# Dilation-16 attention of heads 8 to 15 of layer 0 from stored rows, off TensorE

## The chip, the cores and the metric

One Trainium2 chip; the kernel runs on one core. The metric is device time in microseconds (us), the median of several runs. The kernel before takes 2405.73 us (three runs, 2405.4 to 2406.24).

## What is computed

Four layers run one after the other on x of 256 tokens by 2048 columns (batch 1). Layer 0, which the change touches, is dilated attention with 16 heads of 128 columns and three patterns:

```
DSA_PATTERNS = ((128, 1), (512, 4), (2048, 16))     # (window, dilation)
h = x @ w_in                                        # 2048 x 20480: q, k, v for 3 groups of 2048, then z
for g, (window, dilation) in enumerate(DSA_PATTERNS):
    q = apply_rope(qkv[:, :, g, 0], cos, sin)
    k = apply_rope(qkv[:, :, g, 1], cos, sin)
    o, l = dilated_window_attention(q, k, qkv[:, :, g, 2], window, dilation)   # out, log-sum-exp
wts = jax.nn.softmax(jnp.stack(lses, axis=0), axis=0)
o = jnp.einsum('gbsh,gbshd->bshd', wts, jnp.stack(outs, axis=0).astype(jnp.float32))
y = o.reshape(B, S, DSA_WIDTH).astype(x.dtype) * jax.nn.silu(z)
return y @ w_out
```

Query t of a pattern sees keys t, t-d, t-2d, ... up to its window. With dilation 16 and 256 tokens there are 16 residue classes of 16 tokens each, and causal attention runs inside a class. Weighting three softmaxes by their log-sum-exp is the same as one softmax over the keys of all three patterns together. Layers 1 (latent attention), 2 and 3 are not changed.

## The kernel before, in words

**Projections.** TensorE multiplies float32 data as a high and a low part (float32r): x as xh and xl (both in xx), each weight as whi and wlo. SyncE brings weights in units of 128x4x512 float32 (1 MB) into four buffers `raw`. ScalarE casts a half unit (128x1024) to whi (`split`, L1387), VectorE subtracts it from raw to get wlo (L2030), and TensorE may use the half when wlo is done. Both splits of a half are issued three halves ahead of TensorE (AHEAD = 3); whi and wlo have four buffers. SyncE issues unit u when the wlo of unit u-4 is done.

**Slabs.** The input projection of layer 0 goes by pairs of heads, eight times: six *blocks* (`block_by_rows`, L729 and L730: 256 columns of q or k, weights stationary, result transposed) and two *projects* (`project`, L696 to L698: 512 columns, x stationary), one for v of groups 0 and 1, one for v of group 2 and z. Two banks of PSUM are used in turn. ScalarE copies a slab out (L1636, L1641, L1646), and VectorE adds the part with xl to a block (L2411).

**Work beside the slabs.** All engines walk the same generators: a half is two *steps*, so a block is 8 steps and a project 16. At steps `beside` lets the attention of the pair before run (`heads0`: scores L972, max L2267, exp L1529, transposes L977, product with v L983, result L2385), and from step 54 of a pair's 80 the rotation of the six new blocks (`rope0`), one every three steps: VectorE multiplies by the sine (L2368, twice 64x512), GpSimd by the cosine (L2940, 128x512), VectorE adds (L2372). For one head the scores are two sets (one for each 128 tokens) of 256 + 128 + 128 columns: full block for dilation 1 and the masked 128 of the same half for each of the dilations 4 and 16. Every instruction waits on semaphores, and the order on each engine is as the program is written; nothing is reordered at run time.

The layer ends with the output product (`last_product`), beside which the last pair's heads run.

Of the kernel before, what the change touches and what calls it, by code (L numbers as in the profile page):

```python
# [14 lines left out]
P = 128  # L15
D = 2048
# [23 lines left out]
ROWS_AT = (40, 44, 48, 52)  # L40
# [62 lines left out]
def lanes(gates, delta, lru, gated):  # L103

    lane = [[(0, gates()), (40, lru(0)), (86, lru(2)), (132, delta(0)), (250, delta(2))],
            [(48, lru(1)), (114, lru(3)), (180, delta(1)), (298, delta(3))],
            [(302, gated(0)), (324, gated(1)), (356, gated(2)), (388, gated(3))]]
    tick = 0  # L110
    while any(lane):
        for side in lane:
            if side and tick >= side[0][0] and next(side[0][1], "over") == "over":
                del side[0]
        tick += 1
        yield

# [43 lines left out]
def build_program(nc, a, out, layers=(0, 1, 2, 3)):  # L161
    assert tuple(layers) == (0, 1, 2, 3)
    ctx = ExitStack()
    with ctx:
# [82 lines left out]
        e0_a, s0_d = marks("e0_a", "out*8"), marks("s0_d", "sum*6")  # L247
        p0_a = marks("p0_a", "vb z")
        p0_d = marks("p0_d", "t0 r0 t1 r1 t2 r2 t3 r3 t4 r4 t5 r5 z")
        p0_g = marks("p0_g", "cos*6")  # L250
# [43 lines left out]

        class L0:
            c = Carve()
            h = c(10, TB, HALF)
            t1, t2 = c(2, S), c(2, S)
# [4 lines left out]
            sm, pt, mask = c(TB, N), c(TB, N), c(TB, N)  # L303
            c.at = 14592 + 1152
# [7 lines left out]
            BLOCKS = [(0, 0), (0, 1), (1, 0), (1, 1), (2, 0), (2, 1), (0, 2), (1, 2), (2, 2), (3, 0)]  # L312
# [125 lines left out]

        def xt_turn(layer, g, tb=None):
# [100 lines left out]
        def layers_weights():  # L540
            for pair in range(8):
                cols = [pair * HALF + (3 * g + t) * D for g, t in L0.BLOCKS]
                for c in cols[0:6]:
                    yield from (by_block(L0.w, c, j) for j in range(2))
                for n in (6, 8):
                    yield from (by_columns(L0.w, cols[n:n + 2], j) for j in range(4))
# [67 lines left out]
        def sync(sp):  # L614
            first = [src for _, halves in list(weights())[0:2] for _, src in halves]
            for g in range(8):
                c = slice(g * S, (g + 1) * S)
                sp.dma_start(x[:, :, c], a["x"][0].rearrange("(p t) d -> p t d", t=TB)[:, :, c]).then_inc(x_in[g], 16)
                sp.dma_start(first_piece(raw, g), first[g // 2][:, 2 * (g % 2):2 * (g % 2) + 2]).then_inc(first_in[g], 16)
            for u, (_, halves) in enumerate(weights()):  # L620
# [14 lines left out]
                if u in decays_at:  # L635
# [3 lines left out]
                    sp.dma_start(flat(L3.lane[pair % 2].B), row(decays[2 * pair], 2 * S)).then_inc(dec_in[pair], 16)  # L639
                for dst, src in halves:  # L640
# [10 lines left out]
                if u in ROWS_AT:  # L651
                    q = ROWS_AT.index(u)
                    sp.wait_ge(*xt_p.at(7, "t"))
# [13 lines left out]
        def tensor(pe):  # L667
# [293 lines left out]
            def rope0(pair):  # L961
                yield from turns(7)

            def heads0(pair):
                yield
                for hh in range(2):
                    def scores():
                        for tb in range(TB):
                            for g in range(3):
# [5 lines left out]
                    def turned():  # L975
                        for b in range(8):
                            m = pe.transpose(flat4[:, b * P:(b + 1) * P], L0.sm[:, b // 4, b % 4 * P:(b % 4 + 1) * P], ident[:, :])  # L977
                        return m

                    def pv():  # L980
                        for tb in range(TB):
                            for b, (g, kb) in enumerate(((0, 0), (0, 1), (1, tb), (2, tb))):
                                m = pe.matmul(ps[:, Q + 3, tokens[tb]], L0.pt[:, tb, b * P:(b + 1) * P],  # L983
                                              L0.vb[:, g, kb, hh * P:(hh + 1) * P], start=b == 0, stop=b == 3)
                        return m
                    if hh == 0:
                        pe.wait_ge(*p0_d.at(pair, "r5"))
                    yield from attend(2 * pair + hh, scores, turned, pv, 3, hh == 1)

            def beside0(pair, tables_):  # L990
                return beside(paced(heads0(pair - 1), 3) if pair else tables_, 54, paced(rope0(pair), 3))
# [7 lines left out]
            for pair in range(8):  # L999
                side = beside0(pair, tables())  # L1000
                for s in range(8):
                    if s >= 2:
                        pe.wait_ge(*s0_d.at(pair, f"sum{s - 2}"))
                    elif pair:
                        pe.wait_ge(*e0_a.at(pair - 1, f"out{6 + s}"))
                    if s < 6:
                        block_by_rows(side, bank0(s), pair + s == 0)
                    else:
                        project(side, N, bank0(s),
                                then=turning_y(0, [[hd_d.at(11, "fin"), e0_a.at(7, "out6")]] + 5 * [[]]) if pair + s == 14 else None)  # L1010
                run(side)
            last_product(0, heads0(7), [yt_d.at(5, "lo"), e0_a.all(8)], [], [hd_d.at(15, "fin")])


# [358 lines left out]
        def scalar(act):  # L1373
# [222 lines left out]
            def rope0(pair):  # L1596
                yield from turns(7)

            def heads0(pair):
                act.wait_ge(*e0_a.all(pair + 1))  # L1600
                if pair:
                    act.wait_ge(*hd_p.at(2 * pair - 1, "pv"))
                for g in range(3):
# [4 lines left out]
                act.activation(L0.zs, L0.h[:, 9], ACT.Tanh).then_inc(*p0_a.up("z"))  # L1608
                yield
                for hh in range(2):  # L1610
                    yield from attend(2 * pair + hh, [L0.sm[:, 0], L0.sm[:, 1]], P ** -0.5, flat(L0.pt),
                                      flat4[:, 0:TB * N], 3, hh == 1)

            def beside0(pair, tables_):
                return beside(paced(heads0(pair - 1), 3) if pair else tables_, 54, paced(rope0(pair), 3))
# [10 lines left out]
            for pair in range(8):  # L1626
                side = beside0(pair, tables())
                for s in range(8):
                    b = bank0(s)
                    if s < 6:  # L1630
                        unit(side)
                        unit(side)
                        act.wait_ge(half_done, half[0])
                        if pair:
                            act.wait_ge(*p0_d.at(pair - 1, f"r{s}"))
                        act.copy(L0.h[:, s], ps[:, b:b + 2, 0:S]).then_inc(*e0_a.up(f"out{s}"))  # L1636
                        continue
                    project(side, then=turning_y(0) if pair + s == 14 else None)
                    act.wait_ge(half_done, half[0])
                    if s == 6:  # L1640
                        act.copy(L0.h[:, 6:8].rearrange("p b t c -> p t b c"),  # L1641
                                 ps[:, b:b + 2, :].rearrange("p t (b c) -> p t b c", b=2)).then_inc(*e0_a.up("out6"))
                    else:
                        if pair:
                            act.wait_ge(*p0_d.at(pair - 1, "z"))
                        act.copy(L0.h[:, 8], ps[:, b:b + 2, 0:HALF])  # L1646
                        act.activation(L0.h[:, 9], ps[:, b:b + 2, HALF:N], ACT.Copy, scale=0.5).then_inc(*e0_a.up("out7"))
                run(side)
# [368 lines left out]
        def vector(dve):  # L2017
# [337 lines left out]
            def rope0(pair):  # L2355

                for n in range(6):
                    dve.wait_ge(*s0_d.at(pair, f"sum{n}"))
                    if n == 0:
                        if pair == 0:  # L2360
                            dve.wait_ge(*rope_a.at(0, "tab"))
                            dve.wait_ge(*m0_g.at(0, "same2"))
                        else:
                            dve.wait_ge(*hd_p.at(2 * pair - 1, "sc"))
                    else:
                        dve.wait_ge(*p0_d.at(pair, f"r{n - 1}"))
                    for a_, b_ in ((slice(0, 64), slice(64, P)), (slice(64, P), slice(0, 64))):
                        m = dve.tensor_tensor(L0.t2[a_], L0.h[b_, n], bc(L0.sina[b_], 1, 2), ALU.mult)  # L2368
                    m.then_inc(*p0_d.up(f"t{n}"))
                    dve.wait_ge(*p0_d.at(pair, f"t{n}"))  # L2370
# [3 lines left out]
                yield  # L2374

            def heads0(pair):
                dve.wait_ge(*p0_a.at(pair, "z"))
                dve.scalar_tensor_tensor(out=L0.zs, in0=L0.zs, scalar=1.0, in1=L0.h[:, 9],
                                         op0=ALU.add, op1=ALU.mult).then_inc(*p0_d.up("z"))
                yield  # L2380
                for hh in range(2):
                    def fin(rden):
# [6 lines left out]
                    parts = [(ps[:, Q + tb, :], L0.mask[:, tb], L0.sm[:, tb]) for tb in range(TB)]  # L2389
                    yield from attend(2 * pair + hh, parts, P ** -0.5, fin, 3, hh == 1)  # L2390

            def beside0(pair, tables_):
                return beside(paced(heads0(pair - 1), 3) if pair else tables_, 54, paced(rope0(pair), 3))
# [10 lines left out]
            for pair in range(8):  # L2404
                side = beside0(pair, tables())
                for s in range(8):
                    if s < 6:
                        unit(side)
                        unit(side)
                        dve.wait_ge(*e0_a.at(pair, f"out{s}"))  # L2410
                        dve.tensor_tensor(L0.h[:, s], L0.h[:, s], ps[:, bank0(s):bank0(s) + 2, S:N], ALU.add) \  # L2411
                            .then_inc(*s0_d.up(f"sum{s}"))
                    else:
# [678 lines left out]
```

## Time and profile before

| what | value |
|---|---|
| median of three runs | 2405.73 us |
| span of the profiled execution | 2404.2 us, its ends about 1.5 us inside a run's time |
| TensorE busy | 2395.8 us (100%) |
| VectorE, ScalarE, GpSimd busy | 1478.8, 1186.4 and 151.6 us |
| granted TensorE clock | 1.000 over the span |
| DMA | 418.26 MB, mean 174 GB/s |

A busy time is the time in which an engine had an instruction running. TensorE is the engine to watch: it has an instruction running all the time, so any time it gains or loses is the kernel's. The other engines only matter where they make it wait. In a timeline row the first number is the start, the second the duration, then engine, line, operation, output and inputs, shape, and xN for N instructions merged; square brackets hold idle time before it and who ended it.

### The profile page before, as it was taken

The page shows a single profiled execution, that of the slowest core. Times are in us where ns is not written, and L with a number is a line of the kernel's source. Part 1 is how long each engine was busy: PE and PEld are TensorE (multiplying, and loading weights), DVE is VectorE, ACT ScalarE, POOL GpSimd, SP SyncE. Part 2 cuts the span into 40 slices and gives each one's busy share as a digit, 9 for nine tenths or more (in the row PEclk, how much of TensorE's full clock was granted, in tenths as well). Part 3 has the DMA queues.
Part 4 walks back from the last instruction along what each step waited for, and adds up shares of the span by engine and source line. Part 5 has one row for each costly group of instructions (what it writes and reads, how often), then busy time and mean ns, then how long its engine had stood idle before and what let it go on. Part 6 is the DMA issues. An engine that isn't in the chain of part 4 may idle for free.

```text
span 2404.2 us, 31347 instructions
## 1 busy us (share of the span) xinstructions
PE 2395.8 (100%) x12574; PEld 2043.6 (85%) x12574; DVE 1478.8 (62%) x1986; ACT 1186.4 (49%) x1645; POOL 151.6 (6%) x130
## 2 busy tenths in 40 slices
PE   9999999999999999999999999999999999999999
PEld 8888888888888888878899878888888888888887
DVE  6747575757575757575556576555445566757754
ACT  5454444444444444445455456455444358745543
POOL 0201010101010101000000000000000010000000
PEclk9999999999999999999999999999999999999999
DMA  8555555555555555556654556556555565534344
GB/s 265 178 173 191 196 185 169 186 168 186 168 186 169 186 167 176 194 164 201 188 142 136 193 160 201 179 178 193 177 178 171 175 196 172 157 120 128 126 140 140
DMA packets 370366, 418.26 MB, mean 174 GB/s; under 512 B 28262, under 2 KB 300876, under 8 KB 369708
## 3 DMA queue, kind: packets, MB, share of 16 engines
q1 hardware_dynamic: 368876, 409.36, 53.3%
q0 software_dynamic: 1344, 6.89, 0.8%
q8 instruction: 99, 1.62, 0.3%
q14 instruction: 47, 0.39, 0.0%
HBM read 414.09 MB, written 2.11 MB: 173 GB/s over the span
## 4 chain that ended last, share of the span: by engine, by line
PE 97%; DVE 1%; ACT 1%; issue 0%; POOL 0%; DVEq 0%; ACTq 0%; POOLq 0%
PE ps L696 19%; PE ps L698 19%; PE ps L697 19%; PE ps L730 15%; PE ps L729 7%; PE ps L1260 2%; PE ps L771 2%; PE ps L983 1%; PE ps L972 1%; PE ps L1037 1%; PE ps L1035 1%; PE ps L1036 1%; PE ps L977 1%; PE ps L802 1%; PE ps L804 0%; PE ps L803 0%
## 5 line engine op out<-in xcount | busy, mean ns | idle before, releaser
L2030 DVE TENSOR_TENSOR wlo<-raw,whi 128x1024 fp32r<-128x1024 f32 (+1 forms) x756 | 938.6, 1251 | 617.8 <-ACT whi L1387 615.0
L1387 ACT CAST whi<-raw 128x1024 fp32r<-128x1024 f32 x762 | 789.1, 1041 | 713.8 <-PE ps L698 536.1
L696 PE MATMUL ps<-whi,xx 128*128 128x512 f32 x2060 | 820.3, 398 | 0.0
L698 PE MATMUL ps<-whi,xx 128*128 128x512 f32 x2060 | 803.6, 390 | 0.0
L697 PE MATMUL ps<-wlo,xx 128*128 128x512 f32 x2060 | 802.2, 389 | 0.0
L730 PE MATMUL ps<-xx,whi 128*128 128x512 f32 x1536 | 539.4, 396 | 0.0
L698 PEld LDWEIGHTS ps<-whi,xx 128*128 128x128 f32 x2060 | 386.7, 188 | 82.5
L697 PEld LDWEIGHTS ps<-wlo,xx 128*128 128x128 f32 x2060 | 387.5, 188 | 75.5
L696 PEld LDWEIGHTS ps<-whi,xx 128*128 128x128 f32 x2060 | 387.2, 188 | 74.5
L729 PE MATMUL ps<-xx,wlo 128*128 128x256 f32 x1440 | 406.0, 282 | 0.0
L730 PEld LDWEIGHTS ps<-xx,whi 128*128 128x128 f32 x1536 | 286.3, 188 | 63.2 <-DVE wlo L2030 0.3
L729 PEld LDWEIGHTS ps<-xx,wlo 128*128 128x128 f32 x1440 | 271.6, 189 | 2.5 <-issue 0.5
L2940 POOL TENSOR_TENSOR work<-work 128x512 f32<-128x512 f32 x48 | 96.7, 2014 | 827.6 <-DVE work L2372 627.3
L1529 ACT ACTIVATE work<-work,small 128x128 f32<-128x128 f32 (+1 forms) x80 | 44.4, 555 | 143.2 <-DVE small L2270 143.2
L2368 DVE TENSOR_TENSOR work<-work 64x512 f32<-64x512 f32 x96 | 88.5, 922 | 2.1
L1636 ACT COPY work<-ps 128x512 f32<-128x512 f32 x48 | 28.0, 584 | 60.0 <-PE ps L730 60.0
L2411 DVE TENSOR_TENSOR work<-work,ps 128x512 f32<-128x512 f32 x48 | 32.9, 686 | 36.8 <-ACT work L1636 36.8
L1260 PEld LDWEIGHTS ps<-work 128*128 128x128 f32 x384 | 49.5, 191 | 6.2 <-ACT work L1943 1.6
L1260 PE MATMUL ps<-work 128*128 128x128 f32 x384 | 51.1, 276 | 0.8 <-ACT work L1943 0.4
L2267 DVE CUSTOM_DVE_ANT_0 work<-ps,work 128x128 f32<-128x128 f32 (+1 forms) x80 | 36.0, 487 | 21.0 <-PE ps L972 15.6
L1035 PE MATMUL ps<-xx,whi 128*128 128x256 f32 x160 | 48.1, 301 | 0.0
L1037 PE MATMUL ps<-xx,whi 128*128 128x256 f32 x160 | 45.2, 283 | 0.0
(436 smaller groups left out, 1917.1 us busy)
## 6 DMA issues: line engine op xcount, KB each, us to landing
raw<-in_dsa_w_in SPq DMA_DIRECT2D x316, 512.0 KB, 4.5
raw<-in_ev_w_in SPq DMA_DIRECT2D x144, 512.0 KB, 4.6
raw<-in_od_w_in SPq DMA_DIRECT2D x96, 512.0 KB, 4.6
raw<-in_mla_w_in SPq DMA_DIRECT2D x48, 512.0 KB, 4.5
raw<-in_dsa_w_out SPq DMA_DIRECT2D x32, 512.0 KB, 4.7
raw<-in_mla_w_out SPq DMA_DIRECT2D x32, 512.0 KB, 4.8
raw<-in_ev_w_out SPq DMA_DIRECT2D x32, 512.0 KB, 4.7
raw<-in_od_w_out SPq DMA_DIRECT2D x32, 512.0 KB, 4.9
```

The lines of the kernel that those rows point to most:

```text
L696: pe.matmul(o, xh[:, k, tokens[tb]], hi, start=start and s + l == 0, stop=False)
L697: pe.matmul(o, xh[:, k, tokens[tb]], lo, start=False, stop=False)
L698: m = pe.matmul(o, xl[:, k, tokens[tb]], hi, start=False, stop=stop and s + l == 2)
L729: pe.matmul(ps[:, bank + c, 0:S], lo[:, t, cols], xh[:, k, :], start=False, stop=False)
L730: m = pe.matmul(ps[:, bank + c, :], hi[:, t, cols], xx[:, :, k, :], start=k == 0, stop=k == KT - 1)
L1035: pe.matmul(o, hi, xh[:, k, :], start=first and g != 1, stop=False)
L1037: m = pe.matmul(o, hi, xl[:, k, :], start=False, stop=last and g != 0)
L1260: m = pe.matmul(ps[:, bank, n * P:(n + 1) * P], left[:, n, :], right[:, n, :], start=True, stop=True)
L1387: act.copy(half_of_weights(h)[0][:, :, 0:n] if n > FEW else few_high(h, n), whole_half(raw[:, u % 4, 2 * (h % 2):2 * (h % 2) + 2], n)).the ...
L2030: dve.tensor_tensor(lo[:, :, 0:n] if n > FEW else few_low(h, n), whole_half(raw[:, h // 2 % 4, 2 * (h % 2):2 * (h % 2) + 2], n), hi.bitcas ...
L2368: m = dve.tensor_tensor(L0.t2[a_], L0.h[b_, n], bc(L0.sina[b_], 1, 2), ALU.mult)
L2940: pool.tensor_tensor(L0.t1, L0.h[:, n], bc(L0.cosa, 1, 2), ALU.mult).then_inc(*p0_g.up(f"cos{n}"))
```

## The change

Heads 8 to 15 (pairs 4 to 7) lose their dilation-16 part on TensorE; it is computed once, for all eight heads, on GpSimd and VectorE.

- **Slabs.** After the first block come six new 512-column projects ("row" slabs): q, k and v of group 2 for heads 8 to 15 (1024 columns each). Pairs 4 to 7 have four blocks instead of six, one v project each, and one z project for two pairs. In the whole layer 48 blocks and 16 projects become 40 blocks and 20 projects.
- **Rows.** The q and k rows are rotated in row form on VectorE (`row_ropes`: sine twice 128x512, cosine 128x1024, sum 128x1024, four times), stored to memory (`far_rows`) and read back by `by_sequence` with a partition for each residue class and head (128 of them) and 16 tokens of 128 numbers along it.
- **Products.** For each distance (lag 0 to 15) GpSimd multiplies q and k in pieces of at most 8 tokens (1024 numbers in a partition; 24 pieces, 136 tokens in all), and VectorE sums each piece to its scores. The reduce of piece n stands at step 115 + 6n of the layer. After the exponential (step 260) GpSimd multiplies probabilities and v in the same pieces, and VectorE adds them up at step 279 + 6n. GpSimd's piece n waits for VectorE's piece n-2.
- **Back.** The sums go to memory, come back into y with one maximum and denominator for each token and head, and `attend0` joins them with the other two patterns.
- **Rotation.** In `rope0` the product with the cosine moves from GpSimd to VectorE, for all pairs; it starts at step 150 in pair 0 (which has 176 steps), at 54 in pairs 1 to 3 and at 31 in pairs 4 to 7.
- **Loads of x for the end of the layer** move from units 40 to 52 to units 118 to 130; x holds q, k and v until then.

```diff
+STEPS0 = (176, 80, 80, 80, 64, 48, 64, 48)
+ROPE_AT = (150, 54, 54, 54, 31, 31, 31, 31)
+PIECES = [(lag, n, min(8, LAGS - lag - n)) for lag in range(LAGS) for n in range(0, LAGS - lag, 8)]
+PIECE_STEPS = 6
+FAR_AT, FAR_EXP_AT, FAR_SUM_AT, FAR_OUT_AT = 112, 260, 263, 276
+STORES_AT = {16: 0, 18: 1, 22: 2, 26: 3, 30: 4, 34: 5}
+FAR_LOADS_AT, FAR_VALUES_AT, FAR_STORES_AT, FAR_BACK_AT = 29, 71, 112, 114
...
-                            for g in range(3):
+                            for g in range(3 if pair < 4 else 2):
                                 q, k = L0.qk[:, 2 * g, hh, tokens[tb]], L0.qk[:, 2 * g + 1, hh, tokens[tb] if g else slice(0, S)]
...
                     for a_, b_ in ((slice(0, 64), slice(64, P)), (slice(64, P), slice(0, 64))):
                         m = dve.tensor_tensor(L0.t2[a_], L0.h[b_, n], bc(L0.sina[b_], 1, 2), ALU.mult)
...
-                    dve.wait_ge(*p0_g.at(pair, f"cos{n}"))
-                    dve.tensor_tensor(L0.qk[:, n], L0.t1, L0.t2, ALU.add).then_inc(*p0_d.up(f"r{n}"))
+                    dve.tensor_tensor(L0.t1, L0.h[:, n], bc(L0.cosa, 1, 2), ALU.mult).then_inc(*done.up(f"c{n}"))
+                    dve.wait_ge(*roped0(pair, f"c{n}"))
+                    dve.tensor_tensor(L0.qk[:, n], L0.t1, L0.t2, ALU.add).then_inc(*done.up(f"r{n}"))
                     yield
...
+            def far0():
+                to = steps()
+                for n, (lag, i, size) in enumerate(PIECES):
+                    yield from to(FAR_AT + PIECE_STEPS * n + 3)
+                    dve.wait_ge(*far_g.at(0, f"q{n}"))
+                    dve.tensor_reduce(L0.far_s[:, lag + i:lag + i + size, lag], L0.tmp[n % 2][:, 0:size], AX.X, ALU.add) \
+                        .then_inc(*far_d.up(f"s{n}"))
...
+                for n, (lag, i, size) in enumerate(PIECES):
+                    if lag:
+                        yield from to(FAR_OUT_AT + PIECE_STEPS * n + 3)
+                        o = L0.far_o[:, lag + i:lag + i + size]
+                        dve.wait_ge(*far_g.at(0, f"o{n}"))
...
+                        dve.tensor_tensor(o, o, L0.tmp[n % 2][:, 0:size], ALU.add).then_inc(*far_d.up(f"a{n}"))
...
+            for n, (lag, i, size) in enumerate(PIECES):
+                if n >= 2:
+                    pool.wait_ge(*far_d.at(0, f"s{n - 2}"))
+                pool.tensor_tensor(L0.tmp[n % 2][:, 0:size], L0.far_q[:, lag + i:lag + i + size], L0.far_k[:, i:i + size],
+                                   ALU.mult).then_inc(*far_g.up(f"q{n}"))
```

How the order moves. VectorE in the rotation of pair 0, before: from its first block on, L2030 is the low split, L2368 the sines, L2372 the sum of a rotated block.

```order
L2368 TENSOR_TENSOR work<-work 64x512 x2
L2372 TENSOR_TENSOR work<-work 128x512
L2030 TENSOR_TENSOR wlo<-raw,whi 128x1024
L2368 TENSOR_TENSOR work<-work 64x512 x2
L2372 TENSOR_TENSOR work<-work 128x512
L2030 TENSOR_TENSOR wlo<-raw,whi 128x1024 x2
```

The same place in the changed program (L2189 is the low split, L2530 the sines, L2532 the cosine, L2534 the sum, L2566 the reduce of a piece of GpSimd's products):

```order
L2530 TENSOR_TENSOR work<-work 64x512 x2
L2532 TENSOR_TENSOR work<-work 128x512
L2534 TENSOR_TENSOR work<-work 128x512
L2566 TENSOR_REDUCE work<-y 128x8
L2189 TENSOR_TENSOR wlo<-raw,whi 128x1024
L2530 TENSOR_TENSOR work<-work 64x512 x2
L2532 TENSOR_TENSOR work<-work 128x512
L2534 TENSOR_TENSOR work<-work 128x512
L2189 TENSOR_TENSOR wlo<-raw,whi 128x1024 x2
```

Between the same low splits VectorE now has the cosine product, and at every sixth step a reduce.

GpSimd behind the masks, before (the cosine products of all 48 blocks, then the loads for the layer norm):

```order
L2940 TENSOR_TENSOR work<-work 128x512 x48
L2944 DMA work<-in_ln_g 128x2048
L2945 DMA work<-in_ln_b 128x2048
```

And now (L3203 multiplies q and k):

```order
L3203 TENSOR_TENSOR y<-x 128x1024 x3
L3203 TENSOR_TENSOR y<-x 128x896
L3203 TENSOR_TENSOR y<-x 128x1024
L3203 TENSOR_TENSOR y<-x 128x768
L3203 TENSOR_TENSOR y<-x 128x1024
```

The 48 cosine products are gone, and 24 products of q and k and 24 of probabilities and v, of up to twice their size, stand in their place.

## Rows read from the trace of the kernel before

**Rows 1.** The page: busy time (us, share of the span, instructions), and chain by engine

```profile
PE 2395.8 (100%) x12574; PEld 2043.6 (85%) x12574; DVE 1478.8 (62%) x1986; ACT 1186.4 (49%) x1645; POOL 151.6 (6%) x130
...
PE 97%; DVE 1%; ACT 1%; issue 0%; POOL 0%; DVEq 0%; ACTq 0%; POOLq 0%
```

**Rows 2.** Waits of TensorE, its longest: us in total, times, longest

```profile
PE ps L777 <- POOL ident L2909: 1.6, 1, 1.6
```

**Rows 3.** Timeline of TensorE at the borders of slabs, second pair

```profile
151.59 0.28 PE L732 MATMUL ps<-xx,wlo 128*128 128x256 f32 x1
...
162.89 0.28 PE L732 MATMUL ps<-xx,wlo 128*128 128x256 f32 x1
...
176.74 0.28 PE L732 MATMUL ps<-xx,wlo 128*128 128x256 f32 x1
...
187.84 0.28 PE L732 MATMUL ps<-xx,wlo 128*128 128x256 f32 x1
...
198.91 0.39 PE L696 MATMUL ps<-whi,xx 128*128 128x512 f32 x1
...
242.45 0.39 PE L730 MATMUL ps<-xx,whi 128*128 128x512 f32 x1
```

**Rows 4.** Timeline of TensorE, one head: scores, transposes, product with v

```profile
248.08 1.92 PE L972 MATMUL ps<-work 128*128 128x256 f32 x12
249.75 0.36 PE L729 MATMUL ps<-xx,wlo 128*128 128x256 f32 x1
...
262.34 1.03 PE L977 MATMUL ps<-ident,work 128*128 128x128 f32 x8
263.13 0.36 PE L729 MATMUL ps<-xx,wlo 128*128 128x256 f32 x1
...
267.39 1.95 PE L983 MATMUL ps<-work 128*128 128x128 f32 x16
269.17 1.92 PE L972 MATMUL ps<-work 128*128 128x256 f32 x12
```

**Rows 5.** Timeline of VectorE in the rotation of the second pair

```profile
208.40 1.23 DVE L2030 TENSOR_TENSOR wlo<-raw,whi 128x1024 fp32r<-128x1024 f32 x1 [1.49 <-ACT whi L1387]
209.66 1.39 DVE L2368 TENSOR_TENSOR work<-work 64x512 f32<-64x512 f32 x2
211.08 0.69 DVE L2372 TENSOR_TENSOR work<-work 128x512 f32<-128x512 f32 x1
211.69 1.22 DVE L2030 TENSOR_TENSOR wlo<-raw,whi 128x1024 fp32r<-128x1024 f32 x1
212.94 2.37 DVE L2368 TENSOR_TENSOR work<-work 64x512 f32<-64x512 f32 x2
215.34 0.69 DVE L2372 TENSOR_TENSOR work<-work 128x512 f32<-128x512 f32 x1
...
235.50 4.62 DVE L2030 TENSOR_TENSOR wlo<-raw,whi 128x1024 fp32r<-128x1024 f32 x4
```

**Rows 6.** Timeline of GpSimd: a cosine product beside VectorE, one alone

```profile
211.92 2.14 POOL L2940 TENSOR_TENSOR work<-work 128x512 f32<-128x512 f32 x1 [71.91 <-DVE work L2372]
...
257.11 1.30 POOL L2940 TENSOR_TENSOR work<-work 128x512 f32<-128x512 f32 x1 [23.50 <-DVE work L2411]
```

**Rows 7.** Timeline of TensorE: starts of three halves of that project

```profile
207.07 0.39 PE L696 MATMUL ps<-whi,xx 128*128 128x512 f32 x1
...
215.23 0.39 PE L696 MATMUL ps<-whi,xx 128*128 128x512 f32 x1
...
236.99 0.39 PE L696 MATMUL ps<-whi,xx 128*128 128x512 f32 x1
```

**Rows 8.** VectorE's groups by form: count, busy us, mean ns

```profile
L2528 DVE TENSOR_TENSOR work<-work,small 128x1024 f32<-128x1024 f32 x4 | 4.9, 1219 | 0.0
...
L2521 DVE TENSOR_REDUCE small<-work 128x8 f32<-128x1024 f32 x4 | 4.8, 1210 | 0.0
```

**Rows 9.** DMA issues of two kinds: count, size, median us to landing

```profile
raw<-in_dsa_w_in SPq DMA_DIRECT2D x316, 512.0 KB, 4.5
...
out_x<-x SPq DMA_DIRECT2D x3, 512.0 KB, 6.7
```

More of the change, by code:

```diff
@@ L116, in lanes, with joined @@
         yield
+def joined(n, side, more):
+    for _ in range(n):
+        next(side, None)
+        next(more, None)
+        yield
+    yield from side
 def in_turn(*sides):
@@ L437, in head_scales, with gate0, far_scales @@
             return [small[:, 16 + 8 * (h % 4) + 2 * i:18 + 8 * (h % 4) + 2 * i] for i in range(4)]
+        def gate0(pair):
+            return L0.h[:, 9] if pair < 4 else L0.hz[:, :, pair % 2 * HALF:(pair % 2 + 1) * HALF]
+        def far_scales(h):
+            return [small[:, 64 + 4 * (h % 4) + 2 * i:66 + 4 * (h % 4) + 2 * i] for i in range(2)]
         def xt_turn(layer, g, tb=None):
@@ L975, in turned @@
                     def turned():
[L976 to L977 removed]
+                        n = 4 if pair < 4 else 3
+                        for b in range(TB * n):
+                            m = pe.transpose(flat4[:, b * P:(b + 1) * P], L0.sm[:, b // n, b % n * P:(b % n + 1) * P], ident[:, :])
                         return m
@@ L998, in tensor @@
             keep_warm(1, 3)
[L999 to L1012, printed above, removed]
+            for n, (kind, i, block) in enumerate(slabs0):
+                if n == 0 or pair_of(kind, i) != pair_of(*slabs0[n - 1][0:2]):
+                    if n:
+                        run(side)
+                    side = beside0(pair_of(kind, i))
+                if n >= 2:
+                    pe.wait_ge(*read0(*slabs0[n - 2]))
+                if kind == "block":
+                    block_by_rows(side, bank0(n), n == 0)
+                else:
+                    project(side, N, bank0(n),
+                            then=turning_y(0, [[hd_d.at(11, "fin"), read0(*slabs0[n - 1])]] + 5 * [[]]) if n == len(slabs0) - 1 else None)
+            run(side)
+            last_product(0, heads0(7), [yt_d.at(5, "lo"), n0_a.all(4)], [], [hd_d.at(15, "fin")])
             def norms():
@@ L1625, in scalar @@
                 piece(g)
[L1626 to L1642, printed above, removed]
-                    else:
[L1644 to L1648, printed above, removed]
@@ new lines, in scalar @@
+            for n, (kind, i, block) in enumerate(slabs0):
+                if n == 0 or pair_of(kind, i) != pair_of(*slabs0[n - 1][0:2]):
+                    if n:
+                        run(side)
+                    side = beside0(pair_of(kind, i))
+                if kind == "block":
+                    unit(side)
+                    unit(side)
+                else:
+                    project(side, then=turning_y(0) if n == len(slabs0) - 1 else None)
+                evicted0(kind, i, block, bank0(n))
@@ L2355, in rope0 @@
             def rope0(pair):
-                for n in range(6):
-                    dve.wait_ge(*s0_d.at(pair, f"sum{n}"))
+                done = p0_d if pair < 4 else n0_d
+                for n in range(6 if pair < 4 else 4):
+                    dve.wait_ge(*sum0(pair, n))
                     if n == 0:
@@ L2403, in vector @@
                 piece(g)
[L2404 to L2413, printed above, removed]
-                        project(side, then=turning_y(0) if pair + s == 14 else None)
-                run(side)
+            for n, (kind, i, block) in enumerate(slabs0):
+                if n == 0 or pair_of(kind, i) != pair_of(*slabs0[n - 1][0:2]):
+                    if n:
+                        run(side)
+                    side = beside0(pair_of(kind, i))
+                if kind == "block":
+                    unit(side)
+                    unit(side)
+                    dve.wait_ge(*out0(i, f"out{block}"))
+                    dve.tensor_tensor(L0.h[:, block], L0.h[:, block], ps[:, bank0(n):bank0(n) + 2, S:N], ALU.add) \
+                        .then_inc(*(s0_d if i < 4 else t0_d).up(f"sum{block}"))
+                else:
+                    project(side, then=turning_y(0) if n == len(slabs0) - 1 else None)
+            run(side)
             last_product(0, heads0(7), ALPHA)
```

315 lines of the change are left out of this document (268 added, 47 removed).

## The prediction

> **What bounds the kernel now.** I read the page first: TensorE is busy for 2395.8 of 2404.2 us and carries 97% of the chain of waits [rows 1]. Then its waits: the longest is 1.6 us, at the very start [rows 2]. So the kernel is TensorE's instruction stream, end to end. The change is therefore worth what it takes out of that stream, less whatever new waiting it puts into it, and TensorE can wait for one thing above all in layer 0: the low part of the next half of weights, which VectorE makes. The timelines of TensorE and VectorE say how near that wait already is.
>
> In the project of the second pair TensorE begins a half at 207.07 us [rows 7]. VectorE makes its low split from 208.40 to 209.63 [rows 5], for the half that is three further on, which starts at 215.23 [rows 7]: 5.6 us to spare. Then the rotation begins, and eight splits later VectorE starts one at 235.50, done (a quarter of 4.62 us) at 236.7 [rows 5]; TensorE starts on that half at 236.99 [rows 7]. The 5.6 us have shrunk to 0.3. Eight halves are 236.99 - 215.23 = 21.76 us, 2.72 each; VectorE needed 27.1 us for what it does in them, of the 21.8 + 5.6 = 27.4 it may take. It does not delay TensorE, but nothing is left.
>
> Why so long? One rotation costs 1.42 us of sines (209.66 to 211.08) and 0.61 of sum (211.08 to 211.69), 2.03 in all [rows 5]. The next one's sines take from 212.94 to 215.34, 2.40 us, 0.98 longer, and meanwhile GpSimd multiplies by the cosine (211.92 to 214.06) [rows 5, 6]. That product takes 1.30 us when VectorE is idle [rows 6]. Of the 2.14 us beside VectorE, about a microsecond is waiting for the split that ends at 212.91, and then VectorE waits about a microsecond for GpSimd. So a product of 512 numbers costs a busy VectorE 1.0 us. Eight splits of 1.21, six rotations of 2.03 and five such holds make 9.7 + 12.2 + 5.0 = 26.9 us, against the 27.1 measured: this bookkeeping is right to a few tenths, and I use it below.
>
> The Trainium skill ("SBUF — State Buffer", section "Who interferes with whom") says the same of a VectorE instruction with two inputs in SBUF against a GpSimd instruction that reads SBUF: one has a lock for its whole instruction and the other stands still; a reduce does not take part. The trace agrees on the split and the sines (0.98 us); no row here shows a reduce beside GpSimd. By the page's whole-instruction rule a hold would be the full 1.30 us, which would make the sum below some 2.5 us longer.
>
> **What TensorE loses.** For each of heads 8 to 15 a quarter of the score columns (256 of 1024), two of eight transposes and two of eight products with v go. The three groups take 249.75 - 248.08 = 1.67, 263.13 - 262.34 = 0.79 and 269.17 - 267.39 = 1.78 us [rows 4]; a quarter of each is 0.42 + 0.20 + 0.44 = 1.06, and for eight heads 8.5 us. Eight blocks become four projects, with the same number of weight columns. Blocks without a head beside them take 162.89 - 151.59 = 11.30 and 187.84 - 176.74 = 11.10, two projects 242.45 - 198.91 = 43.54 [rows 3]: 8 x 11.2 - 4 x 21.77 = 89.6 - 87.1 = 2.5 us. Together **-11.0 us**. All of it is on the path, since TensorE never waits.
>
> **What VectorE gets.** In the rotation each block now carries the cosine, 0.69 us by the sum of the same shape [rows 5], and the GpSimd hold of 1.0 goes. With a small allowance for its wait on that product I take 2.75 us for a rotation. Alone that would be 9.7 + 16.5 = 26.2 us in eight halves: 0.7 better than before. But the pieces of the far attention fall into the same steps. A reduce of 1024 numbers takes 1.21 us, an elementwise sum 1.22 [rows 8]: 0.15 us for a token of 128. And each reduce or sum releases GpSimd's next product but one, which VectorE, then behind, runs into. The row gives 0.98 us for 512 numbers, 0.25 a token; I take 0.26. The bounds are 0 (the product falls where VectorE is idle or reducing) and 0.325 (the whole 1.30).
>
> The pieces by step, over the eight halves from the first rotated block, against 27.4 us:
>
> - Pair 0 (steps 150 on): reduces of 8, 5 and 8 tokens, 3.2 us; products of 8, 4 and 8, 5.2. 26.2 + 8.4 = 34.6: TensorE waits 7.2.
> - Pair 1 (230 on): reduces of 4 and 3, 1.05; products of 2 and 1, 0.8. 28.05: 0.7.
> - Pair 2 (310 on): sums of 8 and 5, 2.0; products of 8 and 4, 3.1; a product of 5 that holds back the first split, 0.9. 32.2: 4.8.
> - Pair 3 (390 on): sums of 5, 4 and 3, 1.8; products of 3 and 2, 1.3. 29.3: 1.9.
>
> That is 14.6 us of waiting, from 3.4 with no holds to about 17 with whole ones. Pairs 4 to 7 rotate four blocks each with the far part over (it ends at step 417), so nothing is late there.
>
> Outside the rotations a full piece every six steps asks for three splits (3.6), a reduce (1.2), a hold (2.1) and the sums of blocks (0.5): 7.4 of 8.2 us. That fits, but with 0.8 us to spare, and beside a head VectorE also waits for ScalarE. I add 1 us for such places (0 to 8).
>
> **What else moves.** The row rotations (four times two sines, cosine and sum, 1.4 + 1.2 + 1.2 us) are spread over steps 34 to 78 with a split between the parts, where GpSimd does nothing; each part is under the 5.6 us to spare: nothing. The joined heads have a few more small instructions on VectorE, in pairs where the rotation is shorter by two blocks: nothing. SyncE gets 13 transfers and waits in front of the weights. Its waits are for work that is over eight or more steps (11 us) earlier, by the steps of the program. The transfers cost time only if weights land late: a unit is issued when the splits four units back are done, by the program some six halves (6 x 2.72 = 16.3 us) before ScalarE casts it, and lands in 4.5 us [rows 9]. At unit 29 two loads of 1 MB in rows of 512 bytes go first. A 512 KB store takes 6.7 us with its latency [rows 9]; four times that is 27 us as the worst, and 0 if they overlap like weights. I take 0: only 11.8 us of delay would begin to show in the cast, and a further 5.6 in TensorE.
>
> **Sum.** -11.0 + 14.6 + 1.0 = +4.6 us. The profiled execution spans 2404.2 us with 1.5 around it in the median of 2405.73; both shift alike: **2410 us**. What this kernel's measurement can tell from no change is about 0.2%, 4.8 us: 2400.9 to 2410.5. The forecast is thus a small loss at the upper end of no change.
>
> **Rivals.**
> 1. *The holds do not come* (18%): GpSimd's products fall into gaps and reduces. For it: only half of VectorE's time is taken on average. Against it: in the rotation VectorE has no gap at all [rows 5], and GpSimd is released by VectorE itself. Time: 2405.7 - 11.0 + 3.4 = 2398, faster.
> 2. *GpSimd's pieces are dearer than its cosine products* (10%): with strided rows or a broadcast factor at twice the time, the holds are 0.52 a token. In the rotations 40 tokens more by 0.26 add 10; outside them six steps ask for 9.5 of 8.2 us, 1.3 late on each of some 20 full pieces, about 25. Time: about 2445. It decides from the point where sum and hold of a piece pass 4.1 us. Against it: type and operation are those of rows 6.
> 3. *The far loads delay the weights* (7%): 27 + 4.5 - 21.9 = 9.6 us of waiting at step 112, on top of the rest: 2420. For it: rows of 512 bytes; against it: 2 MB is two units' worth.
>
> **How the numbers follow.** The forecast's own case (65%) spans 2404 to 2417; I give 36% of all to its part within 0.2% and 29% to the part above. With rival 1 nearly all faster (17%, 1% same) and rivals 2 and 3 slower: faster 17%, same 37%, slower 46%. The range from 2398 to 2421 takes in rivals 1 and 3 and the bounds of the holds.
>
> **What would show it.** TensorE's busy share in layer 0 should fall, with waits for the low split (nothing before) near steps 150 to 170 and 310 to 330, some 7 and 5 us, less near 230 and 390. VectorE should be without idle there, with splits and sines of 2 to 3 us beside GpSimd; a product of 1024 numbers on GpSimd should take about 2.4 us alone and 3 to 4 beside VectorE; reduces should keep 1.2. Blocks and projects should keep 11.2 and 21.8 us. The prediction is wrong if TensorE never waits (rival 1), if its waits lie between the rotations (rival 2), or if ScalarE waits for a transfer near unit 29 (rival 3). No row shows TensorE waiting for microseconds, so whether its granted clock then stays at 1.000 is not priced; a fall would add to the loss.

## The result and the profile after

The changed kernel takes **2410.61 us** (18 runs, 2408.82 to 2411.68), the kernel before 2405.89 in the same comparison (18 runs, 2405.33 to 2406.38). The ratio is 1.0019, 95% interval 1.0012 to 1.0025: a loss of 4.7 us, small, but the interval leaves out 1. The forecast was 2410.0. The profiled execution of the changed kernel took 2408.82 us, with a span of 2406.7, and is the quickest of its 18; why most are 1.8 us above it is told with the last experiment.

The page, with the busy times (us, share of the span, instructions) and the chain of waits by engine, beside [rows 1]:

```profile
PE 2387.6 (99%) x12366; PEld 2027.7 (84%) x12366; DVE 1537.5 (64%) x2100; ACT 1181.0 (49%) x1642; POOL 150.2 (6%) x131
...
PE 91%; DVE 5%; issue 2%; ACT 1%; DMA 0%; POOL 0%; SPq 0%; DVEq 0%; ACTq 0%
```

TensorE has less to do than before, by 2395.8 - 2387.6 = 8.2 us, and yet the span is 2.5 us longer. The chain, 97% TensorE before, now runs 5% of the way over VectorE. The longest wait of TensorE (us in total, times, longest), beside [rows 2]:

```profile
PE ps L808 <- DVE wlo L2189: 9.4, 8, 2.3
```

It is new: eight times TensorE stands still for a low split. All eight lie beside the rotations of pairs 0 to 3. The timeline of TensorE shows two of them in pair 0, and below them three groups of matmuls of a head (start, duration, line, tiles, count; in brackets the wait ahead of it):

```profile
210.02 0.39 PE L808 MATMUL ps<-whi,xx 128*128 128x512 f32 x1
...
242.86 0.50 PE L808 MATMUL ps<-whi,xx 128*128 128x512 f32 x1 [1.97 <-DVE wlo L2189]
243.66 0.63 PE L808 MATMUL ps<-whi,xx 128*128 128x512 f32 x1
...
255.21 0.50 PE L808 MATMUL ps<-whi,xx 128*128 128x512 f32 x1 [2.28 <-DVE wlo L2189]
...
260.79 0.39 PE L842 MATMUL ps<-xx,whi 128*128 128x512 f32 x1
...
729.15 1.47 PE L1081 MATMUL ps<-work 128*128 128x256 f32 x8
730.38 0.36 PE L841 MATMUL ps<-xx,wlo 128*128 128x256 f32 x1
...
742.97 0.82 PE L1087 MATMUL ps<-ident,work 128*128 128x128 f32 x6
743.54 0.36 PE L841 MATMUL ps<-xx,wlo 128*128 128x256 f32 x1
...
767.98 1.50 PE L1095 MATMUL ps<-work 128*128 128x128 f32 x12
769.23 0.36 PE L841 MATMUL ps<-xx,wlo 128*128 128x256 f32 x1
```

The two projects of pair 0, from 210.02 to 260.79, last 50.77 us; two such projects, of the second pair, lasted 43.54 in the kernel before [rows 3]. The difference, 7.23 us, is what TensorE loses there. The same reading for pairs 1, 2 and 3 gives 44.53, 47.42 and 45.52: losses of 0.99, 3.88 and 1.98, in all **14.1 us**. It is more than the 9.4 us of idle time. In the stream a matmul starts about 0.23 us after the one before and overlaps it, which a wait undoes; the first matmul after a wait takes longer (0.50 for 0.39 us); and after the first long wait several run slowly (0.63). This duration, less 43.54, is the measure for every experiment below. At the bottom a head's scores now take 1.23 us (1.67 before), its transposes 0.57 (0.79) and its product with v 1.25 (1.78) [rows 4].

VectorE in the rotation of pair 0, beside [rows 5]:

```profile
237.85 2.37 DVE L2530 TENSOR_TENSOR work<-work 64x512 f32<-64x512 f32 x2
...
243.97 1.39 DVE L2530 TENSOR_TENSOR work<-work 64x512 f32<-64x512 f32 x2
245.39 0.69 DVE L2532 TENSOR_TENSOR work<-work 128x512 f32<-128x512 f32 x1
246.12 0.69 DVE L2534 TENSOR_TENSOR work<-work 128x512 f32<-128x512 f32 x1
246.73 1.21 DVE L2566 TENSOR_REDUCE work<-y 128x8 f32<-128x1024 f32 x1
247.85 1.22 DVE L2189 TENSOR_TENSOR wlo<-raw,whi 128x1024 fp32r<-128x1024 f32 x1
249.10 3.47 DVE L2530 TENSOR_TENSOR work<-work 64x512 f32<-64x512 f32 x2
...
253.94 2.35 DVE L2189 TENSOR_TENSOR wlo<-raw,whi 128x1024 fp32r<-128x1024 f32 x2
...
478.98 2.99 DVE L2530 TENSOR_TENSOR work<-work 64x512 f32<-64x512 f32 x2
```

There is no gap. Three sines stand one below the other: 1.39 us alone (243.97), 2.37 beside a product of 512 numbers (237.85), 3.47 beside one of 1024 (249.10). The additions are 0.98 and 2.08 us: a hold. The reduce of 1.21 us and this hold stand in front of the split of 253.94, the first of two, done at about 255.2; TensorE waits for it until 255.21. In the second phase, where GpSimd multiplies by a probability that is repeated over 128 numbers, the addition is 2.99 - 1.39 = 1.60. GpSimd at the same places, beside [rows 6]:

```profile
171.45 2.40 POOL L3203 TENSOR_TENSOR y<-x 128x1024 f32<-128x1024 f32 x1 [6.46 <-DVE work L2566]
...
248.02 3.31 POOL L3203 TENSOR_TENSOR y<-x 128x1024 f32<-128x1024 f32 x1 [9.05 <-DVE work L2566]
...
537.97 1.92 POOL L3210 TENSOR_TENSOR y<-x,work 128x1024 f32<-128x1024 f32 x1 [13.37 <-DVE x L2586]
```

Each is released by VectorE (the reduce L2566, the sum L2586) and so starts just as VectorE goes on with its next split: the one at 248.02 lies about 1.05 us beside the split of 247.85 and ends at 251.33, 2.23 us into the sines of 249.10.

The transfers of the far part: the issues of SyncE from 60 to 200 us (count, size, median us to landing), beside [rows 9]:

```profile
x<-far_rows SPq DMA_DIRECT2D x2, 0.5 KB, 11.4
...
raw<-in_dsa_w_in SPq DMA_DIRECT2D x50, 512.0 KB, 5.5
```

Then, a fence each, SyncE's longest wait for the far part (us, times, longest), its timeline from 105 to 175 us and ScalarE's in the same stretch:

```profile
SPq L706 <- DVE work L2559: 25.6, 3, 14.2
```

```profile
111.70 12.72 SPq L753 DMA_DIRECT2D raw<-in_dsa_w_in  x8
138.72 0.54 SPq L707 DMA_DIRECT2D far_rows<-work  x1
139.31 5.23 SPq L753 DMA_DIRECT2D raw<-in_dsa_w_in  x6
145.35 6.52 SPq L714 DMA_DIRECT2D x<-far_rows  x2
```

```profile
145.90 1.05 ACT L1499 CAST whi<-raw 128x1024 fp32r<-128x1024 f32 x1 [1.89 <-DMA raw<-in_dsa_w_in]
...
162.68 1.05 ACT L1499 CAST whi<-raw 128x1024 fp32r<-128x1024 f32 x1 [2.16 <-DMA raw<-in_dsa_w_in]
```

SyncE, with the weights queued behind, waits 14.2 us until a rotated row can be stored (124.4 to 138.7), sends six transfers of weights at once, and then the two loads of q and k in rows of 512 bytes take its queue for 6.5 us. ScalarE waits twice for weights. The first wait ends about when the loads are issued, so it belongs to the wait for the row; the second can be theirs. Most of the 1.89 and 2.16 us is not delay: the casts beside them, which wait for TensorE, stand idle for 1.67 (beside a project) or 1.77 us (beside a block) as well. By their usual spacing of 2.72 and 2.82 us these two casts are 0.2 and 0.4 us late. TensorE waits for neither.

### The profile page after: what moved, and what is told of

Same layout as the page of the kernel before. It is cut to its first block, busy times and chain, and to the rows that moved or that the text cites. A ratio compares the mean times of both kernels' runs of the same rounds, so it can differ in the third digit from the quotient of the medians.

```text
span 2406.7 us, 31010 instructions
## 1 busy us (share of the span) xinstructions
PE 2387.6 (99%) x12366; PEld 2027.7 (84%) x12366; DVE 1537.5 (64%) x2100; ACT 1181.0 (49%) x1642; POOL 150.2 (6%) x131
## 4 chain that ended last, share of the span: by engine, by line
PE 91%; DVE 5%; issue 2%; ACT 1%; DMA 0%; POOL 0%; SPq 0%; DVEq 0%; ACTq 0%
PE ps L808 19%; PE ps L810 19%; PE ps L809 19%; PE ps L842 12%; PE ps L841 6%; PE ps L1372 2%; DVE work L2530 2%; PE ps L883 2%; DVE wlo L2189 1%; PE ps L1095 1%; PE ps L1081 1%; PE ps L1148 1%; PE ps L1149 1%; PE ps L1147 1%; DVE work L2532 1%
## 5 line engine op out<-in xcount | busy, mean ns | idle before, releaser
L2189 DVE TENSOR_TENSOR wlo<-raw,whi 128x1024 fp32r<-128x1024 f32 (+1 forms) x756 | 949.1, 1263 | 604.4 <-ACT whi L1499 601.8
L808 PE MATMUL ps<-whi,xx 128*128 128x512 f32 x2188 | 872.4, 399 | 9.5 <-DVE wlo L2189 9.4
L810 PE MATMUL ps<-whi,xx 128*128 128x512 f32 x2188 | 854.1, 390 | 0.0
L809 PE MATMUL ps<-wlo,xx 128*128 128x512 f32 x2188 | 852.9, 390 | 0.0
L808 PEld LDWEIGHTS ps<-whi,xx 128*128 128x128 f32 x2188 | 411.5, 188 | 93.7 <-DVE wlo L2189 13.7
L810 PEld LDWEIGHTS ps<-whi,xx 128*128 128x128 f32 x2188 | 411.2, 188 | 87.7
L809 PEld LDWEIGHTS ps<-wlo,xx 128*128 128x128 f32 x2188 | 411.9, 188 | 80.1
L842 PE MATMUL ps<-xx,whi 128*128 128x512 f32 x1280 | 450.0, 396 | 0.0
L842 PEld LDWEIGHTS ps<-xx,whi 128*128 128x128 f32 x1280 | 238.7, 188 | 52.2
L841 PEld LDWEIGHTS ps<-xx,wlo 128*128 128x128 f32 x1200 | 226.5, 189 | 2.0 <-issue 0.3
L3203 POOL TENSOR_TENSOR y<-x 128x1024 f32<-128x1024 f32 (+7 forms) x24 | 51.3, 2139 | 291.6 <-DVE work L2566 157.3
L2530 DVE TENSOR_TENSOR work<-work 64x512 f32<-64x512 f32 x80 | 62.9, 787 | 1.8
L3210 POOL TENSOR_TENSOR y<-x,work 128x1024 f32<-128x1024 f32 (+7 forms) x22 | 40.1, 1822 | 171.8 <-DVE x L2586 171.8
```

Of the source, the lines that this page charges most:

```text
L808: pe.matmul(o, xh[:, k, tokens[tb]], hi, start=start and s + l == 0, stop=False)
L809: pe.matmul(o, xh[:, k, tokens[tb]], lo, start=False, stop=False)
L810: m = pe.matmul(o, xl[:, k, tokens[tb]], hi, start=False, stop=stop and s + l == 2)
L841: pe.matmul(ps[:, bank + c, 0:S], lo[:, t, cols], xh[:, k, :], start=False, stop=False)
L842: m = pe.matmul(ps[:, bank + c, :], hi[:, t, cols], xx[:, :, k, :], start=k == 0, stop=k == KT - 1)
L2189: dve.tensor_tensor(lo[:, :, 0:n] if n > FEW else few_low(h, n), whole_half(raw[:, h // 2 % 4, 2 * (h % 2):2 * (h % 2) + 2], n), hi.bitcas ...
```

## The experiments

Every kernel was compared with the kernel before on the same chip (medians there 2405.9 to 2406.0), and read by the four durations above. Two theories stood against each other at first. *Late VectorE*: the reduces, sums and holds of the far attention make VectorE late inside the rotations. *Late transfers*: the far part's DMAs delay the weights.

**few: all instructions and transfers, hardly any data.**

```
-  pool.tensor_tensor(L0.tmp[n % 2][:, 0:size], L0.far_q[:, lag+i : lag+i+size], L0.far_k[:, i:i+size], ALU.mult)
+  pool.tensor_tensor(L0.tmp[n % 2][:, 0:size, 0:2], L0.far_q[..., 0:2], L0.far_k[..., 0:2], ALU.mult)
   (the reduce, the products with v after lag 0 and the sums likewise on 0:2)
```

> The changed kernel with all far pieces cut from 128 to 2 columns of each token (the dilation-16 part of heads 8 to 15 is left incomplete): GpSimd's products and VectorE's sums shrink to a few hundred ns, TensorE's stream, the slabs and all transfers stay. Theory (VectorE is late in the four rotations because of sums and holds): TensorE no longer waits, 2405.9 - 11.0 = 2395, clock 1.000. Rival A (the loss comes from the far transfers or from the new slabs): no better than 2405, with waits that remain.

Measured: 2394.99 us (2394.69 to 2395.35), ratio 0.9954 [0.9941, 0.9966]. TensorE does not wait for L2189 in any rotation. Against the kernel before on its chip (2406.03) that is -11.0 us, the saving of TensorE as it was worked out, with every transfer of the change still there. Late transfers thus cost TensorE nothing, and the whole loss is in the data that GpSimd and VectorE go through. GpSimd's products take 0.23 us here (16 numbers, VectorE not at a split).

**noholds: only GpSimd's products short.** VectorE keeps its reduces and sums at full length.

```
+  pool.memset(y[:, :, D // 2:D], 0.0)
-  pool.tensor_tensor(L0.tmp[n % 2][:, 0:size], L0.far_q[...], L0.far_k[...], ALU.mult)
+  pool.tensor_tensor(L0.tmp[n % 2][:, 0:size, 0:2], L0.far_q[..., 0:2], L0.far_k[..., 0:2], ALU.mult)
   (the product with v likewise)
```

> Only GpSimd's products are cut to 2 columns (so the far part is wrong); VectorE's sums keep their full size. Theory: sums alone make VectorE 3.4 us too late in all (2.0 in pair 0, under 1 in the others): 2398. Rival B (GpSimd does not matter, VectorE's added work does): TensorE waits nearly as long as in the changed kernel, 2408 to 2410. Rival A: 2410.

Measured: 2399.64 us (2399.38 to 2400.13), ratio 0.9974 [0.9963, 0.9984]. The rotations lose 2.11, 0.45, 0.97 and 0.94 us, 4.5 in all (3.4 expected). The sines at the same piece as above on VectorE, two products of 16 numbers on GpSimd, and TensorE's wait:

```profile
246.15 1.39 DVE L2530 TENSOR_TENSOR work<-work 64x512 f32<-64x512 f32 x2
```

```profile
245.06 1.13 POOL L3205 TENSOR_TENSOR y<-x 128x16 f32<-128x16 f32 x1 [9.15 <-DVE work L2566]
...
256.83 0.23 POOL L3205 TENSOR_TENSOR y<-x 128x16 f32<-128x16 f32 x1 [3.78 <-DVE work L2566]
```

```profile
PE ps L808 <- DVE wlo L2189: 2.9, 5, 0.9
```

The sines that took 3.47 us take 1.39. So the additions are made by GpSimd's products, and without them 14.1 falls to 4.5: the holds are worth 9.6 of the 14.1 us. A product of 16 numbers takes GpSimd 0.23 us when VectorE is not at a split (256.83). The one at 245.06 takes 1.13 because it is held itself: VectorE's split runs from 244.90 to 246.12, the product ends at 246.19, and it holds nothing.

**nosums: only VectorE's reduces and sums short.** GpSimd's products are whole.

```
-  dve.tensor_reduce(L0.far_s[...], L0.tmp[n % 2][:, 0:size], AX.X, ALU.add)
+  dve.tensor_reduce(L0.far_s[...], L0.tmp[n % 2][:, 0:size, 0:2], AX.X, ALU.add)
-  dve.tensor_tensor(o, o, L0.tmp[n % 2][:, 0:size], ALU.add)
+  dve.tensor_tensor(o[:, :, 0:2], o[:, :, 0:2], L0.tmp[n % 2][:, 0:size, 0:2], ALU.add)
```

> Only VectorE's reduces and sums are cut to 2 columns (so the far part is wrong); GpSimd's products keep their full size. Theory: holds alone leave waits of about 4.4, 0, 3.1 and 0.5 us in pairs 0 to 3: 2403. Rival B: 2395. Rival A: 2410.

Measured: 2403.24 us (2401.77 to 2404.64), ratio 0.9987 [0.9978, 0.9996]; in the profiled run the rotations lose 4.48, 0.07, 1.63 and 0.43, 6.6 in all (8 expected). VectorE at the piece of above:

```profile
245.29 0.16 DVE L2566 TENSOR_REDUCE work<-y 128x8 f32<-128x16 f32 x1
...
246.61 3.48 DVE L2530 TENSOR_TENSOR work<-work 64x512 f32<-64x512 f32 x2
```

The reduce is gone and the hold is there as before (3.48). Taking the sums away gives back 7.5 us, taking the holds away 9.6, together 17.1 of 14.1: more than all. Without the pieces a rotation has about 1.2 us to spare (27.4 - 26.2 in the prediction), which absorbs a part of what is left; in the change it counts once, in these two experiments it counts in each.

**gaps: the same pieces at other steps.** The whole computation, every instruction of the change; only the steps at which the pieces stand are others: closer together between the rotations (2 to 5 steps apart where it was 6), and none inside one.

```
-PIECE_STEPS = 6
+PRODUCT_AT = (113, 118, 123, 128, 133, 138, 142, 172, 176, ..., 223, 226, 251, 253)
+SUM_AT = (0, 0, 284, 289, 294, 299, 303, 332, 336, ..., 383, 386, 411, 413)
...
-                    yield from to(FAR_AT + PIECE_STEPS * n + 3)
+                    yield from to(PRODUCT_AT[n])
...
-                        yield from to(FAR_OUT_AT + PIECE_STEPS * n + 3)
+                        yield from to(SUM_AT[n])
```

> The whole computation; only the steps of the far pieces move, so that none stands within a rotation: as close as 5 steps for 8 tokens, 2 for one, in steps 113 to 142, 172 to 226, 251 to 253, and for the sums 284 to 303, 332 to 386, 411 to 413. Theory: TensorE does not wait in the rotations, since those alone ask for 26.2 of 27.4 us; time about 2395, at most 2398 if a head and close pieces meet. Rival A or B (work in total, wherever it stands): 2408 to 2411.

Measured: **2395.05 us** (2394.95 to 2395.43), ratio 0.9954 [0.9942, 0.9967]. It beats both kernels: by 11.0 us the one before on its chip, by 15.6 the change (difference of the medians). All four durations are 43.52 us, the loss is zero. VectorE in the rotation, and TensorE's longest wait:

```profile
239.40 1.39 DVE L2531 TENSOR_TENSOR work<-work 64x512 f32<-64x512 f32 x2
...
246.16 4.85 DVE L2190 TENSOR_TENSOR wlo<-raw,whi 128x1024 fp32r<-128x1024 f32 x4
250.93 0.81 DVE L2567 TENSOR_REDUCE work<-y 128x5 f32<-128x640 f32 x1
```

```profile
PE ps L890 <- POOL ident L3175: 1.6, 1, 1.6
```

The sines take 1.39 and the reduce comes after the last splits. Outside a rotation VectorE bears a piece every two to five steps without making TensorE wait: it was not too much work, but work at the wrong steps.

With the pieces so close, one reduce lies wholly beside a product of GpSimd. First VectorE, then GpSimd:

```profile
304.01 1.22 DVE L2567 TENSOR_REDUCE work<-y 128x8 f32<-128x1024 f32 x1
```

```profile
303.04 3.06 POOL L3204 TENSOR_TENSOR y<-x 128x896 f32<-128x896 f32 x1 [5.19 <-DVE work L2567]
```

The reduce takes 1.22 us, as it does alone: beside a product this reduce is not held, as the sines are.

**half: only the second phase moved.** The table SUM_AT of *gaps*; the first phase stays at every six steps.

> The changed kernel with the sums of the second phase moved out of the rotations (steps 284 to 303, 332 to 386, 411 to 413) and the reduces of the first phase left where the change has them. Theory: the losses of pairs 0 and 1 stay (7.2 and 1.0 us), those of pairs 2 and 3 go: 2395 + 8.2 = 2403. Rival B (total work): 2408 to 2410.

Measured: losses 7.24, 1.01, -0.03, -0.02. Pairs 0 and 1 lose what they lose in the change, pairs 2 and 3 nothing: the phases act apart, each in its own rotations. The profiled run takes the time expected, 2402.74 us, the median is 2404.8 (2402.74 to 2405.65), ratio 0.9995 [0.9986, 1.0003].

**pace4: the change with the rotated blocks four steps apart.**

```
-  paced(rope0(pair), 3)
+  paced(rope0(pair), 4 if pair < 4 else 3)
```

> The changed kernel with the rotations of pairs 0 to 3 spread, one every four steps instead of three; pieces as in the change. Theory, by the same bookkeeping with splits 1.21, rotation 2.75 and holds of 0.26 (first phase) or 0.2 us a token (second phase): VectorE too late by 4.1 us in pair 0, about 1.2 in pair 2, nothing in pairs 1 and 3: 2395 + 5.3 = 2400. Rival D (the pieces, not how close the rotations are, set the loss): as the changed kernel, 2410.

Measured: 2401.0 us (2400.67 to 2401.82), ratio 0.9979 [0.997, 0.9988]; losses 3.05, -0.02, 0.78, -0.02. More time for the same work removes most of the loss. A part moves on: after the rotations of pairs 0 and 2 TensorE waits in the next block (0.6 and 0.9 us, the second line). The blocks after these two rotations take 0.8 and 1.2 us longer than in *few*, so 5.8 us are lost in all where 5.3 were expected.

```profile
PE ps L808 <- DVE wlo L2189: 2.2, 4, 1.0
...
PE ps L841 <- DVE wlo L2189: 1.5, 2, 0.9
```

**cosine: the kernel before, with that one part of the change.** The cosine product goes to VectorE, GpSimd's loop of 48 products goes away.

```
-  dve.wait_ge(*p0_g.at(pair, f"cos{n}"))
+  dve.tensor_tensor(L0.t1, L0.h[:, n], bc(L0.cosa, 1, 2), ALU.mult).then_inc(*p0_d.up(f"c{n}"))
```

> The kernel before with one part of the change alone: the cosine product of the rotation moves from GpSimd to VectorE. Theory (a rotation on VectorE then takes 2.75 us instead of 2.03 and a hold of 1.0, so it ends 0.7 us earlier): no change, 2405.9, no waits of TensorE. Rival C (the cosine on VectorE is part of the loss): slower, 2407 or more, with waits for the low split at the end of each rotation.

Measured: 2405.87 us, ratio 0.9999 [0.999, 1.0008]; no waits in the rotations. VectorE:

```profile
208.54 1.23 DVE L2030 TENSOR_TENSOR wlo<-raw,whi 128x1024 fp32r<-128x1024 f32 x1 [1.49 <-ACT whi L1387]
209.79 1.39 DVE L2368 TENSOR_TENSOR work<-work 64x512 f32<-64x512 f32 x2
211.21 0.69 DVE L2370 TENSOR_TENSOR work<-work 128x512 f32<-128x512 f32 x1
...
234.84 4.84 DVE L2030 TENSOR_TENSOR wlo<-raw,whi 128x1024 fp32r<-128x1024 f32 x4
```

From 208.54 to 234.84 are 26.3 us; in the kernel before it was 235.50 - 208.40 = 27.1 [rows 5]. Doing 0.69 us more for each block makes VectorE 0.8 us quicker over eight splits, because a hold of 0.98 goes with each cosine product that leaves GpSimd.

**again: the change, profiled a second time,** because its first profiled run was quicker than all its others.

> The changed kernel once more, for a second profile: its first one, at 2408.8, is the fastest of its 18 runs, most are near 2410.6. Theory: here the granted clock falls once more, after a wait behind which VectorE is no longer late, and that costs about 1.7 us; waits for the low split stay about 10 us in all. If instead another wait appears or one is longer, it is VectorE again.

Measured: 2410.63 us, span 2408.5. The waits are the same to 0.04 us, but pair 0 loses 8.85 us instead of 7.23; pairs 1 to 3 lose 1.02, 3.91 and 1.95. TensorE in two stretches of pair 0, one after each long wait, first in the run of above, then here (stretch, its length, busy time, granted clock, share and GB/s of the DMAs):

```profile
245.00:250.00 5.00, 5.00 (x19) 0.79 0.45 158
...
258.00:261.00 3.00, 3.00 (x15) 1.00 0.92 318
```

```profile
245.00:250.00 5.00, 5.00 (x20) 0.84 0.48 169
...
258.00:261.00 3.00, 3.00 (x10) 0.62 0.94 325
```

In both, the granted clock falls after the first long wait (1.97 us); only here it falls again after the second (2.29 us), which this timeline shows:

```profile
255.34 0.50 PE L808 MATMUL ps<-whi,xx 128*128 128x512 f32 x1 [2.29 <-DVE wlo L2189]
...
257.22 0.63 PE L809 MATMUL ps<-wlo,xx 128*128 128x512 f32 x1
257.65 0.63 PE L810 MATMUL ps<-whi,xx 128*128 128x512 f32 x1
```

Here, from one matmul's start to the next is 0.43 us instead of 0.23, nearly twice the time: the lower of the two levels, 1.2 instead of 2.4 GHz. Some eight matmuls by 0.2 us are the 1.6 us. In the runs' times the same step can be seen. The kernels whose longest wait for a low split is 2.3 us or more (the change, nosums, half) spread over 2.9 us each, and the ten other runs of half lie 1.8 us or more above its profiled one; those with 1.0 us at most (few, noholds, gaps, pace4) spread over 0.5 to 1.2. In nosums the mean granted clock of the runs goes with the time: 1.000 in the five runs of 2401.8 to 2402.1 us, 0.999 in the six of 2403.2 to 2404.6. What decides whether the clock falls stays open. The length of the wait alone does not decide it: in the profile of nosums the clock stays at 1.00 behind a wait of 2.84 us, and in that of half it falls behind the one of 1.96 and not behind the one of 2.27.

## Why the prediction was right

The account closes: 2405.9 before, -11.0 saved (few), +14.1 in the rotations is 2409.0, against 2408.8 of the profiled run; the second fall of the clock, 1.6, makes 2410.6, the median.

- **TensorE's saving, -11.0.** Right, measured apart by *few*. Only the sum is measured so: by the rows of one head it saves 4.24 [rows 4] - 3.05 = 1.19 us rather than 1.06, which would leave the blocks less than the 2.5 forecast. The -11.0 also holds something that the prediction took to be alike: a run of the changed kernel takes 2.1 us more than its span (2408.82 - 2406.7), one of the kernel before 1.5 to 1.8. By the spans (2404.2 and 2392.9) *few* saves 11.3.
- **Late in the rotations, +14.6.** Right: 14.1. Pair by pair 7.2, 0.99, 3.88 and 1.98, where 7.2, 0.7, 4.8 and 1.9 were forecast. The mechanism held too: noholds, nosums and gaps each take about as much of the loss away as the part was to have (4.5 us left for 3.4 expected, 6.6 for 8, none for none), and *cosine* confirms the starting point, 0.7 us back in eight halves (0.8 measured).
- **The hold.** Forecast 0.26 us a token, from one row of 512 numbers; measured 2.08 for 8 tokens, 0.26. It is less than the whole product (2.40 alone). Of the product at 248.02, 2.26 us lie behind the end of the split (249.07 to 251.33), and the sines lose 2.08 of these; why not all is not shown. The sentence of the Trainium skill ("SBUF — State Buffer", section "Who interferes with whom"), by which the loser stands still for the whole instruction, agrees that the sines, with two inputs in SBUF, are held, and is some 0.3 us too dear here (2.40 against 2.08). The reduce in *gaps* agrees with what the prediction takes from the same section, that a reduce does not take part. With probabilities as a factor the hold is 1.60, 0.20 a token, as the product takes 1.92 alone. The forecast used 0.26 there too, which fits with pair 2 being 0.9 dearer in it than on the chip.
- **Other places, +1.0.** Not there. Outside the rotations TensorE does not wait once for a low split, and *gaps* shows that even two to five steps for a piece are enough.
- **The clock, not priced.** It costs 1.6 us in one of two profiles, after the last long wait of pair 0; the runs' times suggest the same for most executions. The fall after the first wait costs nothing of its own: VectorE's splits, not TensorE, then set the end of the projects, so slower matmuls only fill time that would be waited: at 255.21 TensorE had caught up and waited again. The 1.0 for other places that was not there and the 0.5 too much in the rotations cover this 1.6 nearly to the tenth: the forecast's 2410.0 is closer to 2410.6 than its terms deserve.
- **Transfers, 0.** Right for TensorE, wrong on the way there. SyncE's waits were taken to be for work long done, but one of 14.2 us stood in front of the weights, past the 11.8 us from which the forecast let a delay show in the casts. Two casts were then 0.2 and 0.4 us late, far less than the 5.6 us that the splits are ahead of TensorE.
- **Rivals.** *Holds do not come* is refuted by the sines of 3.47 us, *dearer pieces* by the absence of waits between the rotations (2.40 us alone is 1.85 times the 1.30 for half the numbers [rows 6]), and *far loads* by few.

## What to carry to other kernels

Where an engine that feeds the bottleneck has a lead that shrinks and grows, new work beside it is priced by place: sum up what stands in the stretch where the lead is smallest, holds by the other engine included, and compare with lead and time there; an average busy share (64% here) says nothing. If the sum doesn't fit, first move the work to the steps where the lead recovers: the same instructions went from a loss of 4.7 us to a gain of 11. A wait of 2 us on TensorE may cost more than itself, since the clock can fall after it.

## What the runs showed of the hardware beyond that

- After waits of about 2 us in an otherwise full stream TensorE's granted clock fell to the lower level for a few microseconds (matmuls every 0.43 instead of 0.23 us), but not each time: after the first of two waits in both profiles of the change, after the second in one of them only, and after neither in the profile of nosums (1.05 and 2.84 us). The kernels with waits of 1.0 us at most show no such spread between runs.
- Two loads of 1 MB in rows of 512 bytes kept SyncE's queue for 6.5 us at their issue and landed after 11.4 us (median), against 5.5 for weights of 512 KB in the same stretch.
- A product of 16 numbers a partition took GpSimd 0.23 us, one of 1024 numbers 2.40 us, and one of 1024 with a factor that is repeated along the row 1.92. Released beside VectorE's split, the first took 1.13 and the second 3.31: the hold goes both ways.
